# Six of eleven feature pairs of the down projection by the seven-product form

## The reference

```python
D_FF = ((8 * D_MODEL // 3 + 255) // 256) * 256      # 2816
def swiglu(h, wg, wu, wd):
    return (jax.nn.silu(h @ wg) * (h @ wu)) @ wd
...
        f = swiglu(h, p['w_ffn_gate'][l], p['w_ffn_up'][l], p['w_ffn_down'][l])
        x = x + g_f * rmsnorm(f, p['norm_ffn_post'][l])
```

## Time and profile before

| | |
|---|---|
| three runs, us | 2963.36, 2962.05, 2953.34 (median 2962.05) |
| the profiled execution, us | 2957.34, of which its span 2955.6 |
| PE busy | 2791.9 us, 94% of the span, 24793 matmul records |
| DVE / ACT / POOL busy | 1757.3 / 1074.0 / 1195.7 us (59 / 36 / 40%) |
| mean granted TensorE clock | 0.972 |
| DMA | 377.86 MB, mean 128 GB/s |

### The profile page before, as it was taken

How to read it: one execution, slowest core, us unless ns; L and a number is a source line. 1 busy time by engine, 2 the same in 40 slices (tenths; PEclk the granted TensorE clock), 3 DMA queues, 4 the chain that set the end, 5 groups by cost and what they waited for, 6 DMA issues and landing times. The chain is left out here.

```text
span 2955.6 us, 60037 instructions
## 1 busy us (share of the span) xinstructions
PE 2791.9 (94%) x24793; PEld 2546.5 (86%) x24793; DVE 1757.3 (59%) x3048; ACT 1074.0 (36%) x2145; POOL 1195.7 (40%) x822
## 2 busy tenths in 40 slices
PE   6999999999998989999999998898999999999997
PEld 4887776666668989999999987878988999999997
DVE  5341245588874776666652277976487666664235
ACT  4511026522224643333320045765553333331012
POOL 2411137733315634444432134784544444443111
PEclk7999999999998999999999998999999999999999
DMA  9546400177753312323264233101332322346322
GB/s 301 203 166 216 138 20 4 43 285 272 269 182 96 120 67 89 118 89 103 104 247 169 94 98 112 42 29 44 92 102 82 104 103 95 112 153 233 133 96 87
DMA packets 232394, 377.86 MB, mean 128 GB/s; under 512 B 14522, under 2 KB 155195, under 8 KB 223668
## 3 DMA queue, kind: packets, MB, share of 16 engines
q1 hardware_dynamic: 200108, 253.95, 25.8%
q0 software_dynamic: 11776, 75.50, 7.1%
q10 hardware_dynamic: 20240, 44.57, 4.1%
HBM read 298.71 MB, written 73.28 MB: 126 GB/s over the span
## 5 line engine op out<-in xcount | busy, mean ns | idle before, releaser
L805 PE MATMUL ps<-HS,w_split 128*128 128x272 f32 x1920 | 272.5, 292 | 20.1 <-POOL w_split L1402 9.8
L805 PEld LDWEIGHTS ps<-HS,w_split 128*128 128x128 f32 x1920 | 252.9, 190 | 26.2 <-ACT sg L1067 14.4
L821 PE MATMUL ps<-HS,w_ring 128*128 128x272 f32 x1920 | 273.6, 289 | 0.0
L821 PEld LDWEIGHTS ps<-HS,w_ring 128*128 128x128 f32 x1920 | 254.3, 189 | 0.0
L2370 PEld LDWEIGHTS ps<-HS_in,w_split 128*128 128x128 f32 x1728 | 222.9, 191 | 27.3 <-issue 16.4
L1787 DVE TENSOR_TENSOR Y<-Y,ps 128x272 f32<-128x272 f32 x256 | 112.1, 438 | 224.7 <-PE ps L821 224.7
L2370 PE MATMUL ps<-HS_in,w_split 128*128 128x272 f32 x1728 | 233.9, 294 | 8.7 <-DVE HS_in L2590 8.6
L1402 POOL TENSOR_TENSOR w_split<-w_raw,w_split 128x512 fp32r<-128x512 f32 x120 | 170.4, 1434 | 154.3 <-ACT w_split L1059 154.3
L776 PE MATMUL ps<-HS,w_ring 128*128 128x272 f32 x1344 | 178.8, 294 | 17.7 <-PEq L3508 10.5
L776 PEld LDWEIGHTS ps<-HS,w_ring 128*128 128x128 f32 x1344 | 174.5, 192 | 20.3 <-POOLq L1438 10.7
L1402 POOL TENSOR_TENSOR w_ring<-w_raw,w_ring 128x512 fp32r<-128x512 f32 x40 | 62.6, 1564 | 269.5 <-ACT w_ring L1059 269.5
(11 more groups left out here) (517 smaller groups left out, 6346.2 us busy)
## 6 DMA issues: line engine op xcount, KB each, us to landing
hid_spill<-hid SPq DMA_DIRECT2D x40, 1088.0 KB, 7.4
w_mod_half<-w_mod_in SPq DMA_DIRECT2D x40, 1024.0 KB, 6.4
HS<-hid_spill ACTq DMA_DIRECT2D x32, 1088.0 KB, 10.5
w_raw<-w_ffn_gate_in SPq DMA_DIRECT2D x44, 512.0 KB, 4.2
w_raw<-w_ffn_up_in SPq DMA_DIRECT2D x44, 512.0 KB, 4.3
w_raw<-w_ffn_down_in SPq DMA_DIRECT2D x44, 512.0 KB, 4.6
x_part<-x_spill SPq DMA_DIRECT2D x54, 272.0 KB, 3.1
x_spill<-Y SPq DMA_DIRECT2D x12, 1088.0 KB, 5.7
```

Source lines behind the costliest of these rows:

```text
L805: ins = pe.matmul(psum(U.banks(u)[b]), part_slot(j, a)[:, k, :], token_part(n, j, e)[:, k, :], start=(j < 3 and k == 0 and i == 0), stop=( ...
L821: ins = pe.matmul(down_bank(n), slots[DOWN_SLOT[t]][:, a, d * P:(d + 1) * P], hid_cols(k, t, q)[:, e, :], start=(t == lo and j == 0), stop ...
```

## The change

Rows 6 to 17 of w_ffn_down (blocks f = 3 to 8, PAIRS, twelve rows) leave the plain chunks; these become (0, 2), (2, 4) and the closing six rows. The six blocks are multiplied by seven products each. Two blocks at a time are summed in PSUM: a pass p has two blocks (k = p // 2) and one token half (n = p % 2), seven products i, four banks d, 6 matmuls for each bank (halved). Six passes stand between the plain chunks and the closing one. DVE adds each product to Y or to shared_rows (add_product; two banks in one instruction) and the shared sums at the end (merge).

The weight sums of a block are made on DVE (row_sums, two) and POOL (row_difference, two), the high parts on ACT (row_high, seven for each block) and the low parts on POOL (row_low, seven), in pieces of 128 x 512, into 20 half slots (ROW_BLOCK) that are reused when the product that read them is done (block_free).

The token sums are made of the hidden values behind each up unit: four subtractions on DVE (hidden_sums), four high parts on ACT (sums_high), four low parts on POOL (sums_low), into one set of buffers in Y's last quarter, and from there by two transfers to memory (store_sums, part_spill). The hidden values of these blocks that are needed themselves are three of four. They are stored by four transfers instead of one.

```diff
-CHUNKS = ((0, 2), (2, 4), (4, 8), (8, 12), (12, 16), (16, 22))
+CHUNKS = ((0, 2), (2, 4), (4, 10))
...
+PAIRS = tuple(range(3, NFG - 2))
+NPASS = len(PAIRS)
+SUM_ORDER = ((0, 2), (2, 0), (1, 3), (3, 1))
...
         def load_last(eng, n):
             for p in range(2):
                 eng.wait_ge(first_out[p], 64)
-            eng.wait_ge(hid_out, 16 * U.hid_stores(NFG - 1))
+            eng.wait_ge(hid_out, 16 * U.stores(END))
+            eng.wait_ge(prod, S_END - (0 if n else 4 * NPROD))
...
+            def store_sums(u):
+                m, f, mat, n = U.UNIT[u]
+                to = part_spill[(f - PAIRS[0]) // 2, n]
+                sp.wait_ge(sum_lo, 4 * U.summed(u) + 4)
+                for a in range(2):
+                    sp.dma_start(to[:, a, 2:6, (f - PAIRS[0]) % 2, :], y_r[:, 4 * a:4 * a + 4, qs(3)].bitcast(F32)
+                                 ).then_inc(sum_out, 16)
...
+            def load_pair(m):
+                for u in range(2):
+                    if m == 0:
+                        sp.wait_ge(down_lo, 3 + u)
+                    else:
+                        sp.wait_ge(part_lo, NPROD * (NBATCH + m))
...
+            sp.wait_ge(prod, S0)
             load_hid(sp, 1)
             store_hid(END - 1)
-            for t in range(4, NROWS):
+            load_pair(0)
+            load_pair(1)
...
+            for p in range(3, NPASS):
+                load_pair(p)
+                for h in range(2):
+                    load_tokens(p, h)
+            load_last(sp, 0)
+            for t in range(CHUNKS[NCHUNK][0], NROWS):
                 load_down(t)
+            load_last(sp, 1)
...
+            def halved(p, i):
+                f = NPROD * p + i
+                k, n = p // 2, p % 2
+                pe.wait_ge(part_lo, NPROD * (NBATCH + 2 * k + 1) + i + 1)
+                if i % 4 == 0:
+                    pe.wait_ge(tokens_in[n][i // 4], 32 * k + 32)
+                for d in range(KH):
...
+                    for u in range(2):
+                        for j, (a, e) in enumerate(((0, 0), (0, 1), (1, 0))):
+                            ins = pe.matmul(psum(product_bank(p, i, d)), row_part(2 * k + u, i, a)[:, d * P:(d + 1) * P],
+                                            token_cols(n, i, u, e), start=(i in (0, 1, 4, 5) and u == 0 and j == 0),
+                                            stop=(i in (2, 3, 5, 6) and u == 1 and j == 2), skip_group_check=True)
...
                    act.wait_ge(prod, NPROD * u + 4)
                     if U.held(u):
                         act.wait_ge(hid_lo, U.held(u))
+                        if U.UNIT[u - 2][1] in PAIRS:
+                            act.wait_ge(sum_lo, 4 * U.summed(u - 1))
...
+            def sums_high(u):
+                m, f, mat, n = U.UNIT[u]
+                for x, (i, s) in enumerate(SUM_ORDER):
+                    act.wait_ge(sum_made, 4 * U.summed(u) + x + 1)
+                    if x == 0 and U.summed(u):
+                        act.wait_ge(sum_out, 32 * U.summed(u))
+                    act.activation(sum_high(s), gate_buf(U.gate_of(u), i), ACT.Copy).then_inc(sum_hi, 1)
...
+                late = u - 1 if u >= 1 and U.UNIT[u - 1][2] and U.UNIT[u - 1][1] in PAIRS else None
...
+                if late is not None and n:
+                    sums_high(late)
                 finish(2)
                 finish(3)
+                if late is not None and not n:
+                    sums_high(late)
...
             for m in range(1, NBATCH):
                 for j in range(NPROD):
                     part_low(m, j)
+                if m >= 2 and U.BATCH[m - 1][1] and U.BATCH[m - 1][0] in PAIRS:
+                    for u in (U.FIRST[m - 1], U.LAST[m - 1]):
+                        sums_low(u)
...
+            def hidden_sums(u):
+                b11, b22, b12, b21 = (gate_buf(U.gate_of(u), i) for i in range(4))
+                n = 4 * U.summed(u)
...
+                dve.tensor_tensor(b11, b12, b11, ALU.subtract).then_inc(sum_made, 1)
+                dve.wait_ge(sum_made, n + 1)
+                dve.tensor_tensor(b12, b22, b12, ALU.subtract).then_inc(sum_made, 1)
...
+            def row_sums(m):
+                for u in range(2):
+                    dve.wait_ge(part_in[u], 16 * (NBATCH + m) + 16)
...
+                dve.tensor_tensor(s1_down[:, :], a21, a22, ALU.add).then_inc(sums_made, 1)
+                dve.tensor_tensor(a21, a11, a21, ALU.subtract).then_inc(sums_made, 1)
...
                     if (k, h) == (0, 1):
                         for i in range(4):
                             hidden_low(U.PAIR0, i)
-                        dve.wait_ge(hid_lo, 8 * NFG)
+                        dve.wait_ge(hid_lo, 8 + U.lows(END))
+                        row_sums(0)
                     for d in range(KD):
+                        if (k, h, d) == (1, 0, 5):
+                            row_sums(1)
                         for q in range(2 * h, 2 * h + 2):
                             take(k, d, q)
```

281 lines of the change are left out of this document (229 added, 52 removed).

## The result

The change makes the kernel slower: 3075.6 us (median of 4 runs, 3075.3 to 3079.6) against 2961.4 for the kernel before, a ratio of 1.040 with a 95% interval of 1.0385 to 1.0413 (the two medians alone give 1.0386). That is 114 us more; 49 more were forecast (3010, range 2970 to 3050). The direction was right, and the size lies outside the range.

A forecast was written before the change was run, and what follows sets the result against it. PE was taken to set the pace in the gate and up units and the down projection. -36.1 + 51.6 + 9.6 + 17.0 + 7 = +49 on 2957.3 or 2962 gave 3010 us, range 2970 to 3050.

The forecast's parts named there:

- Fewer matmuls: Down projection: 1008 matmuls in place of 1152 per layer at 125.4 ns each, -36.1 us in both layers.
- Token sums at the block ends: Gate and up units: PE loses 4.3 us at each of 12 block ends, +51.6 us; high bound 86.
- lies inside the 4.3: Block end: the stall of the sigmoid and DVE's product sums adds nothing to PE's 4.3 us loss.
- DVE's sums: After the first up unit: four subtractions at 0.47 less one hidden_low, 1.5 us later; PE stands about 0.7.
- Start of the down projection: PE stands 4.8 us a layer while row_sums(0) waits for weight rows, +9.6 us in both; high end 8 a layer.
- if the rows land like the store beside them (7.4): Start of the down projection: condition for the high end, PE standing 8 us a layer.
- The closing chunk: End of the down projection: PE waits 8.5 us a layer for six rows (6.4 to 10.7), +17.0 us in both.
- The clock: Low clock after the two long waits in each layer, about 1.7 us each, +7 us.
- The short ones at the block ends I leave at nothing: Clock loss after the short waits at block ends was put at nothing; the high end was to hold it.
- the fourth, contention: Block ends: DVE's sums and POOL's low parts hold each other up, also costing clock; +96, 3058 us, chance 0.12.
- the first, the whole gain: Down projection's gain comes through whole, with the sums' store wait and closing rows covered; 2926 us, chance 0.09.

The follow-up runs named there:

- no_sums_sp: Changed kernel without token sums (plain quarters stored), first weight-row pair loaded before the last hidden store, most closing rows before the last tokens: 2924.7 us, ratio 0.9888.
- no_sums: Changed kernel with all token sums of the hidden products left out, plain quarters stored in their place: 2969.3 us, ratio 1.0047.
- pool_order: Changed kernel with POOL taking the sums' low copies earlier and SP storing the first unit's sums ahead of the next parts load: 3075.2 us, ratio 1.0393.
- pool_no_sub: pool_order with DVE's subtractions also left out, so plain quarters are stored as sums: 2993.6 us, ratio 1.0124.
- sp_start: Changed kernel with only the first pair of down projection weight rows loaded ahead of the last hidden store: 3057.6 us, ratio 1.0342.
- dve_pool: pool_order with DVE's subtractions also spread behind multiplies of the next unit, none of the second unit's ahead of add_b: 3011.0 us, ratio 1.0184.
- lows_add_first: Changed kernel, all work kept, engine and SP orders rearranged, sums' low copies on DVE, add_b and add_e ahead of two part sums: 2942.3 us, ratio 0.9939.

## Why the prediction was right in direction and wrong in size

**Fewer matmuls, -36.1.** Right: no_sums_sp is 34.6 under the kernel before.

**Token sums at the block ends, +51.6.** This is the step that failed: 104 by the periods and 104 to 106 by no_sums, above its high bound of 86. The prediction followed one chain (POOL's copies, the store, copy_a) to product 3 of the second gate unit and took the lateness there, 4.3 us, as the whole price of a block end. Three parts of that were wrong.

First, the chain itself was priced too low. From the end of POOL's part 6 (1207.21 + 2.71 = 1209.9) to the start of product 3 (1224.24) are 14.3 us. Before it was 1248.3 to 1257.02, 8.7. So this chain cost 5.6, not 4.3; the store, seen by ACT 8.9 us after its issue (1213.62 to 1222.52), had been put at 6.2, and the 1.5 us for DVE did not come on this path. Another 0.6 had come up before that point: part 6 ended 7.7 us after the start of the block's first shown product, and 7.1 before. That makes product 3 6.2 us late. The store lies behind a weight load and the hidden stores here; in pool_order, where the first unit's store goes out ahead of the load, the median of these 544 KB transfers is 4.1 us, against 6.0 in the changed kernel. The Trainium skill (DMA: Bandwidth & Descriptors, Anatomy of one DMA, the two cost components) has the fit cited in the prediction, measured on the GpSimd path; as an estimate it gives about 4.6 for these bytes, and the trace, with 8.9, does not agree.

Second, the sentence that the stall of the sigmoid and of DVE's product sums "lies inside the 4.3, since copy_a comes later still". Without its last wait of 0.93 on copy_a, PE would still have come to product 3 about 5.1 us late, by the waits of 1.14 on copy_a and 2.70 on add_b and by 1.6 of clock. This hold is nearly as long as the chain. It adds little while the chain ends later, and it is the reason why mending the chain alone gains nothing.

Third, behind the chain's end the prediction had nothing, and the rest, 3.2 us, comes there: the second unit's low copies on POOL ahead of part 0 push the part sum, add_22 (1.33) and one more copy_a (0.28), and the 0.66 on add_b comes on top; each such stop costs PE about 0.26 more than its wait. Together 9.4, the growth of this block.

Which hold is "the" cause has no answer by subtraction. Take DVE's out, and 1.7 us a block are gained; change POOL's and SP's order, and 0.4 are; both, 6.8 (pool_no_sub). The prediction's chain does exist, and PE waited 2.5 to 3.8 us for it once DVE was no longer first.

**DVE's sums, 1.5 us, in which PE lost 0.7.** The 0.66 on add_b of the second up unit (1249.90) is that 0.7. But the price of 0.47 for each subtraction held for operations without POOL beside them. The second unit's took 4.65 us for four and stand ahead of add_b; the prediction had priced the first unit only. It had cited the stretch in words and put it into the high bound alone. The Trainium skill (GPSIMD Engine Reference, section 1, Specifications) says that VectorE instructions with two SBUF inputs contend with GpSimd, and the trace agrees: 1.34 and 1.38 with POOL at work, 0.44 without, in pool_order.

**Start of the down projection, +9.6.** The mechanism was right, and the size was its high end: PE stood 7.80 and 8.0 us against 4.8 taken and 8 as bound, and with the restart 9 a layer (sp_start). PE stopped where the prediction said, six sums after DVE's last bank. The mis-sized terms are the second row's landing, some 6.8 us after its own issue (the longest of these loads) instead of 4.6, and the first row sum, 1.17 beside a POOL operation instead of 0.68. The case of the high end, "if the rows land like the store beside them (7.4)", nearly came about.

**The closing chunk, +17.0.** Mechanism right again; waits of 13.2 and 15.0 instead of 8.5, over the bound of 10.7, and 27 us in both layers with the clock. The chain of six rows was as read (21.5 to 20.8). The landing of the first row was not: 10.4 us from its issue, behind the four transfers of the closing chunk's hidden values, where 4.6, or at most 8.6, had been put.

**The clock, +7.** Right for the long waits: after them the granted clock was 0.50 for 3.7 us (from 1578.34) and 4.2 us (from 1751.52), 1.8 and 2.1 lost where 1.7 each had been put. "The short ones at the block ends I leave at nothing" was wrong: behind the 2.70 us the loss was 1.5 us a block in the mean of six, some 18 in all. The granted clock over 310 us fell to 0.97, and it is 1.00 in dve_pool, whose waits are 1.7 at most. How much of the 104 is clock, beside waits, is only read from these rows; no experiment held the one fixed.

**The rivals.** None gave the time. The nearest was the fourth, contention, 3058: its two features (subtractions and low copies hold each other up; clock is lost at the block ends) were both there. Of the first, the whole gain, one can now say where its time would lie: 2925, at no_sums_sp.

What stays open: in lows_add_first the token sums still cost some 2 us a block (44.78 to 42.68), spread over waits of 1.4 us at most in the stretch shown. I did not find which of DVE's operations it is.
